# A transformer pair on one core: the recurrent scan as a pipeline over pairs of heads, fewer columns in 16 linear tiles, and the last projection computed by rows

## The reference

```python
def _wkv7_scan(r, w, k, v, a, b):          # 16 heads of 64, over 272 tokens
    def step(S, inp):
        sa = einsum('bhvk,bhk->bhv', S, a_t)
        S = S * w_t[:, :, None, :] + sa[..., None] * b_t[:, :, None, :] + v_t[..., None] * k_t[:, :, None, :]
        return S, einsum('bhvk,bhk->bhv', S, r_t)
...
z_rwkv = z_rwkv + (z_prev - z_rwkv) * mu           # r, k, v and three small inputs
y_b = _fox(z_fox, q_g, k_g, f_bias)                # softmax attention with a decay bias
merged = g_a * (y_a @ w_a) + g_b * (y_b @ w_b)
h = h + merged @ w_o
gate, up = jnp.split(_rms(h, n2) @ w_gu, 2, axis=-1)
return h + (jax.nn.silu(gate) * up) @ w_dn         # the last projection, "down2"
```

## Time and profile before

| | us |
|---|---|
| median of three runs (2892.56 to 2895.17) | 2893.81 |
| the profiled execution | 2892.87 |
| its span | 2890.8 |
| PE busy in the span | 2856.2 |
| DVE busy | 1735.4 |
| ACT busy | 1223.3 |
| all waits of PE in the view of waits (15 rows) | 27.1 |

### The profile page before, as it was taken

One profiled execution on the slowest core, in us unless ns is written; L12 is line 12 of the kernel. 1 busy time (PEld: TensorE's weight loads), 2 busy tenths in 40 slices (PEclk: granted clock), 3 DMA queues, 4 the chain that ended last, 5 costly groups with the idle time before them and its releaser, 6 DMA issues.

```text
span 2890.8 us, 55153 instructions
## 1 busy us (share of the span) xinstructions
PE 2856.2 (99%) x23517; PEld 2629.2 (91%) x23517; DVE 1735.4 (60%) x2522; ACT 1223.3 (42%) x1788; POOL 53.0 (2%) x102
## 2 busy tenths in 40 slices
PE   9999999999999999999999999999999999999999
PEld 8999998888888999899888888899998888889999
DVE  6467757656566444754666665766666566655444
ACT  5345544333333344633433333455453333334343
POOL 1000000000000000000000000000000000000000
PEclk9999999999999999999999999999999999999999
DMA  7666445565555555455434335445555555555553
GB/s 245 199 168 167 156 163 172 177 190 187 188 189 175 190 187 189 153 167 168 118 88 118 102 89 160 132 123 184 180 186 188 182 183 187 189 189 183 182 188 131
DMA packets 370328, 485.21 MB, mean 168 GB/s; under 512 B 12359, under 2 KB 181654, under 8 KB 370150
## 3 DMA queue, kind: packets, MB, share of 16 engines
q1 hardware_dynamic: 362752, 471.55, 51.6%
q0 software_dynamic: 4112, 7.88, 0.9%
q10 hardware_dynamic: 3302, 3.39, 0.4%
HBM read 475.76 MB, written 7.01 MB: 167 GB/s over the span
## 4 chain that ended last, share of the span: by engine, by line
PE 91%; DVE 6%; issue 1%; ACT 1%; DMA 1%; DVEq 0%; SPq 0%; ACTq 0%
PE psum L338 20%; PE psum L344 12%; PE psum L342 12%; PE psum L343 12%; PE psum L340 10%; PE psum L543 6%; PE psum L547 5%; PE psum L545 5%; DVE w_lo L328 2%; PE psum L1796 1%; DVE arena L716 1%; PE psum L1782 1%; DVE arena L704 0%; PE psum L2612 0%; DVE act L791 0%
## 5 line engine op out<-in xcount | busy, mean ns | idle before, releaser
L328 DVE TENSOR_TENSOR w_lo<-w_raw,w_hi 128x1024 fp32r<-128x1024 f32 x728 | 859.0, 1221 | 797.6 <-ACT w_hi L319 797.6
L319 ACT ACTIVATE w_hi<-w_raw 128x1024 fp32r<-128x1024 f32 x728 | 731.4, 1052 | 1161.8 <-PE psum L340 591.5
L338 PE MATMUL psum<-act,w_hi 128*128 128x512 f32 x2816 | 989.6, 394 | 8.9 <-issue 4.5
L342 PE MATMUL psum<-act,w_hi 128*128 128x256 f32 (+2 forms) x3024 | 854.7, 283 | 6.9 <-issue 4.5
L344 PE MATMUL psum<-act,w_lo 128*128 128x256 f32 (+2 forms) x3024 | 855.6, 283 | 0.0
L343 PE MATMUL psum<-act,w_hi 128*128 128x256 f32 (+2 forms) x3024 | 855.6, 283 | 0.0
L340 PE MATMUL psum<-act,w_lo 128*128 128x256 f32 x2816 | 790.7, 281 | 0.0
L338 PEld LDWEIGHTS psum<-act,w_hi 128*128 128x128 f32 x2816 | 529.6, 188 | 136.8 <-DVE w_lo L328 11.2
L342 PEld LDWEIGHTS psum<-act,w_hi 128*128 128x128 f32 (+1 forms) x3024 | 571.6, 189 | 11.3 <-issue 8.3
L344 PEld LDWEIGHTS psum<-act,w_lo 128*128 128x128 f32 (+1 forms) x3024 | 572.2, 189 | 0.0
L343 PEld LDWEIGHTS psum<-act,w_hi 128*128 128x128 f32 (+1 forms) x3024 | 568.4, 188 | 0.1
(11 more groups left out here) (391 smaller groups left out, 1584.8 us busy)
## 6 DMA issues: line engine op xcount, KB each, us to landing
w_raw<-w_in SPq DMA_DIRECT2D x128, 1024.0 KB, 5.7
w_raw<-w_down SPq DMA_DIRECT2D x88, 1024.0 KB, 5.0
w_raw<-w_gate_up SPq DMA_DIRECT2D x88, 1024.0 KB, 5.0
w_raw<-w_gate SPq DMA_DIRECT2D x44, 1024.0 KB, 5.2
w_raw<-w_up SPq DMA_DIRECT2D x44, 1024.0 KB, 5.2
w_raw<-w_out SPq DMA_DIRECT2D x16, 1024.0 KB, 5.0
w_raw<-w_o SPq DMA_DIRECT2D x16, 1024.0 KB, 5.0
w_raw<-w_branch_a SPq DMA_DIRECT2D x8, 1024.0 KB, 5.0
```

Of the source, the lines that this page charges most:

```text
L319: nc.scalar.activation(w_hi[:, s % 2, 2 * h:2 * h + 2, 0:wd], w_raw[:, s % RAW, 2 * h:2 * h + 2, 0:wd], ACT.Copy).then_inc(hi_ready, 1)
L328: nc.vector.tensor_tensor(w_lo[:, s % 2, 2 * h:2 * h + 2, 0:wd], w_raw[:, s % RAW, 2 * h:2 * h + 2, 0:wd], w_hi[:, s % 2, 2 * h:2 * h + 2, ...
L338: pe.matmul(dst.rearrange("p (h n) -> p h n", h=2), w1, both_parts, start=first, stop=False, skip_group_check=True)
L342: pe.matmul(dst, w1, act_hi[:, k, tok], start=first, stop=False, skip_group_check=True)
```

## The change

The scan becomes a pipeline over pairs: x, u, y of pair j - 1 stand between the products of the inverse of pair j, and an epilogue does those of pair 7. The Gram matrices with r and with k are made behind the joins, the part that the joins need is made small beside the blocks ("near"). Tokens, decay factors and the inverse have two buffers. In the scan ACT now copies u. r and its decayed form take the place of r and k in `z`. Tiles of r ("rkv", the first eight) get 258 columns in place of 272, the first eight fox tiles 256. The last projection keeps the activations stationary and moves 512 weight columns, with the residual added by a float32 matmul against the identity.

The diff, cut to its core:

```diff
+        R_TOK = slice(META - 2, TOK)
+        def r_tiles(lin, i):
+            return lin is L["rkv"] and isinstance(i, int) and i < 2
...
+        def fox_tok(t):
+            return X if t < 8 else ALL
...
+        def rows_pe(lin, lo_base):
+            def residual(s):
+                for b in range(2):
+                    for j in range(4):
+                        pe.matmul(psum[:, 2 * s + b, j * P:(j + 1) * P],
+                                  res[:, 4 * s + j, META + b * P:META + (b + 1) * P], ident,
+                                  start=j == 0, stop=False, skip_group_check=True)
...
+                for s in range(4):
+                    if first:
+                        if s < 2:
+                            pe.wait_ge(acc_free, lin.t0 - 2 + 2 * s)
+                        residual(s)
+                    pe.wait_ge(lo_ready, 2 * u + 2)
+                    for b in range(2):
+                        for k in range(UNIT_K):
+                            pe.matmul(out_rows, x1, w1, start=False, stop=False, skip_group_check=True)
+                            pe.matmul(out_rows, x1, w0, start=False, stop=False, skip_group_check=True)
+                            mm = pe.matmul(out_rows, x0, w1, start=False, stop=last and k == UNIT_K - 1,
+                                           skip_group_check=True)
...
+            def gram_r(j, c):        # bh by r alone: 128 columns for a half, where gram(0, c) had 256
+                for h, r in enumerate(hs):
+                    pe.matmul(o[low], bh[r, t0:t1], r_of[r, t0:t0 + P], start=True, stop=True)
...
+                side(4)
+                if j:
+                    pe.wait_ge(*rd.after(("x128", before)))
+                    pe.wait_ge(*ra.after(("x128", before)))
+                    pe.wait_ge(*rd.after(("gram_r", before)))
+                    front(j)
+                side(4)
...
                 product(4, n8t, n8, "p2")
-                gram(0, 0)
+                if j:
+                    chunk_x(before, 0)
                 dve("ip2")
                 product(5, ip2, i8t, "r1t")
                 act("p2")
                 product(4, p2t, p2, "p4")
-                gram(0, 1)
+                if j:
+                    chunk_u(before, 0)
                 dve("ip4")
                 act("r1t")
                 product(4, r1t, ip4, "s8")
-                gram(1, 0)
+                if j:
+                    act("near")
+                    chunk_y(before, 0)
                 dve("s8t")
                 product(5, nm16, s8t, "v16")
-                gram(1, 1)
+                side(1)
                 act("v16")
                 product(4, v16, s8, "s16")
-                side(1)
+                if j:
+                    chunk_x(before, 1)
                 dve("s16t")
                 product(5, nm32, s16t, "v32", 4)
-                side(1)
+                if j:
+                    chunk_u(before, 1)
                 act("v32")
                 product(4, v32, s16, "s32", 4)
-                side(1)
+                if j:
+                    chunk_y(before, 1)
...
-            down_pe(L["down2"], LO_BASE["down2"], lambda s: s > 1 and end_transpose(s - 2))
-            end_transpose(2)
-            end_transpose(3)
+            rows_pe(L["down2"], LO_BASE["down2"])
```

More of the change, by code:

```diff
@@ L1590, in zt, with ar_of @@
             return z[:, n, 1:ZP]
+        def ar_of(j):
+            return z[:, j:j + 9:8, 1:ZP]
         lora_w = (LORA, LORA, P, P)
@@ new lines, in chunk_x @@
+            def chunk_x(j, c):
+                toks = toks_s[j % 2]
+                pe.wait_ge(*rd.after((f"sh{c + 1}", j)))
+                pe.wait_ge(*rd.after(("gram_k", j)))
+                for h in range(2):
+                    pe.matmul(psum[:, 0, hs[h]], gm[:, 2 * h + c, 2 * P:3 * P], toks[:, 2 + c, hs[h]],
+                              start=h == 0, stop=False, skip_group_check=True)
+                pe.matmul(psum[:, 0, 0:P], ar_of(j)[:, 0, PIECES[c + 1]], state_h.rearrange("p h v -> p (h v)"),
+                          start=False, stop=True, skip_group_check=True) \
+                    .then_inc(*rp.did((f"x{c + 1}", j)))
@@ L1792, in product, with center @@
+            def center(j):
+                pe.wait_ge(*rd.after(("ys", j)))
+                pe.matmul(psum[:, 2, 0:SEQ], T["head_center"], ys, start=True, stop=True) \
+                    .then_inc(*rp.did(("yc", j)))
+            front(0)
+            for j in range(8):
+                before = j - 1
+                inv_t = inv_ts[j % 2]
+                dve, act = lambda n: pe.wait_ge(*rd.after((n, j))), lambda n: pe.wait_ge(*ra.after((n, j)))
                 def product(bank, l, r_, step, nq=5):
@@ L1843, in rwkv_pe @@
                 mm.then_inc(*rp.did(("x64", j)))
+                dve("x0")
+                for h in range(2):
+                    mm = pe.matmul(psum[rows32(h), 2, 0:RHD], s16[rows32(h), 4], xs[rows32(h), 0],
+                                   start=True, stop=True)
+                mm.then_inc(*rp.did(("u0", j)))
+                if j:
+                    pe.wait_ge(*rd.after(("ys", before)))
+                gram_r(j, 0)
+                gram_r(j, 1)
                 side(1)
-                low, high = slice(0, 64), slice(64, P)
                 dve("x64t")
@@ L2026, in rwkv_act, with copy, u_copy @@
             table(ACT.Tanh)
+            def copy(dst, src):
+                return s.activation(dst, src, ACT.Copy)
+            def u_copy(j, c):
+                s.wait_ge(*rp.after((f"u{c}", j)))
+                copy(us, psum[:, 1, 0:P].rearrange("p (h v) -> p h v", h=2)).then_inc(*ra.did((f"u{c}", j)))
             for j in range(8):
@@ L2052, in rwkv_act @@
                 ins.then_inc(*ra.did(("toks", j)))
-                side(6)
-                def copy(dst, src):
-                    return s.activation(dst, src, ACT.Copy)
+                side(7)
                 def evac(step, of, dst, bank, nq=5):
```

637 lines of the change are left out of this document (371 added, 266 removed).

## The result

The changed kernel took 2912.27 us (median of 4 runs, 2905.82 to 2916.43) beside 2893.18 us for the kernel before (4 runs, 2890.67 to 2895.17). The ratio is 1.006, its interval 1.0042 to 1.0077: slower, where 2885 us (2874 to 2895) was predicted. All readings are of the execution of 2905.82 us, span 2903.7; before it was 2892.9 and 2890.8, so 12.9 us of span have to be found. It is the shortest of the four, with a mean granted clock of 0.991 over the execution; the longest, 2916.43 us, has 0.988, so the time of one program moves with its clock.

A forecast was written before the change was run, and what follows sets the result against it. PE, under way for 99% of the span, was taken as the bound. Scan -13, columns -5.1, last projection +0.3 and fox +9 gave -8.8: 2892.9 to 2884.1 us profiled, 2885 against the median, range 2874 to 2895.

The forecast's parts named there:

- The clock: Low clock expected only after the idle stretch at fox's end, with matmuls twice as far apart, priced at 1.7 us.
- the three rivals: Fox's end costs only 3 us (chance 0.2); pairs save only entries (0.2); joins stand open, kernel at 2904 (0.1).
- The pairs: Scan: each pair 2.0 us shorter, 16 us for eight, from entries, exits, grams and small groups, less new waits.
- Entries and exits: Scan, per pair: 11 fewer slot bursts save 1.16 us; fewer changes of shape after slots save 0.28.
- The other 0.3 for the grams and 0.3 for the ends of small groups: Scan, per pair: halved gram calls less "near" save 0.3 us; merged small groups without drains save 0.3.
- New waits: Scan joins, chunks replacing slots and grams: 0.6 us of idleness a pair against 0.4 before, 0.2 more.
- the second rival: Scan: pairs save only the entries, 1.0 to 1.2 us a pair; 2892 in all, no change; chance 0.2.
- The edges of the scan: Pair 0's open joins and pair 7's chunks behind it, less what pairs 0 and 1 lack: net 3 us dearer.
- The end of fox: Pair 7 of fox lacks slots: waits 6.7 us late, second unit 0.5, low clock 1.7; +9 us in all.
- Columns: Narrower tiles save 2.4 us in r and 2.7 in fox; -5.1 us together (-4 to -6).
- The last stage: Last projection: main matmuls -3.6 us, residual +7.6, transposes -1.8, end -1.8; together +0.3 (-3 to +3).
- The third part: Last projection: transposes no longer needed save 1.8 us, and a shorter end saves 1.8.

The follow-up runs named there:

- experiment 1: Changed kernel with six of the ten slots around pair 0's blocks moved into its open joins; 2898.22 us, ratio 1.0015.
- experiment 6: experiment 5 with pair 7's four slots ahead of the inverse moved into its joins; 2886.38 us, ratio 0.9971.
- experiment 5: Changed kernel with six slots back in pair 0's joins and 0 instead of 2 slots behind each fox output; 2890.25 us, ratio 0.9997.
- experiment 9: Kernel before with only the edits outside the scan: columns of r and fox, and rows of the last stage; 2885.09 us, ratio 0.9971.
- experiments 2 and 3: Changed kernel with pair 0's six joins filled with unused work: full-array matmuls (2), 2907.57 us; 32 by 32 matmuls (3), 2921.22 us.
- experiment 11: The changed kernel itself, unaltered, measured once more; 2903.06 us, ratio 1.0034.

## Why the prediction was wrong, by its own steps

**The clock, the step that failed most.** The prediction read the 99% of the earlier trace rows as a PE that stays fast whatever the order, priced a low clock at 1.7 us in fox's end, and let pair 0's joins stand open for 3.0 us of plain waiting. The open joins cost 9.1 us (experiment 1), of which some 8 are the clock; pair 7's stretch and the next 4.2 (experiment 6 beside 5, both stages). The prediction also took matmuls at the lower level as twice as far apart, where they are 1.8 times. With the clock the scan is +9.7 us; without these 12.2 us it would be -2.5. The had shown that PE at 1.2 GHz is 5 us of waiting away, and the same reading was not applied to the joins. None of the three rivals had it.

The Trainium skill, TensorE: Matmul & The Clock Gate, section "What's actually happening", says that the clock gate follows how busy the array has been. The traces agree if busy is not read as the share of time that PE is under way: at the beginning of fox in experiment 1 the clock falls at 1813.74 behind 10.00 us of 10.00 under way (clock: third from the end).

```profile
1803.74:1813.74 10.00, 10.00 (x75) 7.92 (x74) 5.48 (x13) 6.12 (x6) 0.00 (x0) 1.00 0.41 107
1813.74:1817.15 3.41, 3.41 (x18) 3.41 (x18) 0.41 (x2) 0.63 (x1) 0.00 (x0) 0.50 0.59 155
```

What ends just before it are 3.2 us of float32 matmuls with 16 or 128 moving columns. Within the pairs, in contrast, every fall had 0.87 us or more of idle time in the 5 us before it.

**The pairs: -2.0 us each, measured -0.5.** Compare pairs 1 to 6 in experiments 5 and 9, which differ only in the order of the scan and are both at full clock (sums of the intervals from start to start, all six pairs):

```
                                  old order   new order    a pair
slots, entries and exits              159.9       150.0     -1.64
products                               22.2        22.5     +0.05
x: L1939 / L1905                       5.26        5.94     +0.11
x: L1941 / L1907                       2.35        4.44     +0.35
u: L1948 / L1916                       4.35        7.06     +0.45
grams, with near                       14.2        14.2      0.00
all others                             61.0        62.0     +0.17
all                                   269.2       266.1     -0.51
```

Entries and exits were right: 126 bursts became 60, 1.64 us where 1.44 was forecast. But the chunks took 0.91 back, and the prediction had only 0.57 for the changes of shape, hidden in the term "exits". The timeline of PE, changed kernel, pair 2:

```profile
1512.54 0.52 PE L1958 MATMUL psum<-arena 32*32 32x32 f32 x36
1512.99 0.66 PE L1905 MATMUL psum<-arena 128*128 128x64 f32 x4
1513.49 0.44 PE L1907 MATMUL psum<-arena 128*128 128x128 f32 x2
1513.86 0.85 PE L1958 MATMUL psum<-arena 32*32 32x32 f32 x72
1514.63 0.66 PE L1916 MATMUL psum<-arena,tab 128*128 128x64 f32 x4
1515.22 0.52 PE L1958 MATMUL psum<-arena 32*32 32x32 f32 x36
```

x takes 0.50 + 0.37 = 0.87 us between products, u 0.59; behind a slot they took 0.39 + 0.20 and 0.36. A full-array group between two 32 by 32 groups pays on both sides, some 0.1 going in and 0.17 coming out. The other 0.3 for the grams and 0.3 for the ends of small groups did not show. New waits were small, as predicted (PE's idle time in these six pairs is 1.0 us in experiment 5 and 1.7 in 9). This is the second rival's result ("the pairs save only the entries", 1.0 to 1.2 us a pair), reached by another road and at half its size.

**The edges of the scan** were forecast as 3 us dearer. Pair 0, which now has no chunk, is 4.1 us shorter in experiment 5 than in 9 when its five more slots (3.5 us) are put apart, and pair 7's chunks outside cost 16.2 (65.3 - 49.1) - 7.8 (11 slots) - 3.5 (clock, experiment 6) = 4.9: +0.8 net with pair 0's joins filled, where the forecast's 3 us were for open ones.

**The end of fox: +9 us, measured +9.0.** Timeline of PE, changed kernel:

```profile
1951.37 0.87 PE L2830 MATMUL psum<-tab,inv 128*128 128x144 f32 x4
...
1958.93 1.11 PE L2856 MATMUL psum<-arena 16*64 16x256 f32 x4 [4.89 <-ACT arena L2731]
...
1965.56 0.65 PE L2856 MATMUL psum<-arena 16*64 16x256 f32 x4 [1.46 <-ACT arena L2725]
...
1967.34 0.58 PE L342 MATMUL psum<-act,w_hi 128*128 128x256 f32 x1 [0.32 <-DVE act L833]
```

The count of slots, the wait of 4.9 us for the copy of the weights (7.56 us behind scores(7), where 7.5 were forecast from the earlier trace rows), the second wait and the low clock all came as written. Another 1.7 us of low clock fell on "branch".

**Columns: -5.1 us, right.** The part ahead of pair 0 is 2.7 us shorter; by the forecast's price it would be 3.3, 2.4 for r and 0.9 for the 20 fox slots that stand there. The other 44 narrower slots lie in pairs 0 and 1, which experiment 9 has 2.2 us shorter than before (1.9 forecast). Its pairs 2 to 6 are another 1.9 us shorter with the same columns, 1.3 of it idle time of PE.

**The last stage: +0.3 us, measured -2.9.** The main matmuls were mis-sized. Before, 256 columns start 0.1185 us apart, the mean over the stage, not 0.1179 as the earlier trace rows gave; after, 512 start 0.232 apart, as forecast: 5.4 us less, where 3.6 was taken. The residual is cheaper: four times 1.70 us, 6.8 in place of 7.6. The timeline of PE at its first step:

```profile
2648.39 1.95 PE L695 MATMUL psum<-tab,res 128*128 128x128 f32 x16
2650.09 0.48 PE L716 MATMUL psum<-w_hi,act 128*128 128x512 f32 x1
```

The third part, the transposes and the end, came to 4.3 us for its 3.6.

**The sum by these terms**: -13 became +9.7, -5.1 became -4.6, +0.3 became -2.9, +9 became +10.7 with the echo on "branch". With the scan's 12.2 us of clock out, the change would have stood at +0.7, no change (an estimate). The clock alone doesn't bridge the way to -8.8: the pairs' 1.5 us each, 9 us in six of them, are the other step that failed.

## What to carry to other kernels

On a PE-bound kernel, ask of every reordering what the array sees for the next microseconds, not only how many microseconds of queue it saves: wide matmuls between small-tile products do two jobs, covering waits and keeping the clock up, and a stretch left without them can make the slots behind it cost 1.8 times as much. Price a group by its neighbours on both sides; a burst saved is worth nothing if a group of another shape takes its place. Reorderings that move the clock should be tried one at a time: here some 20 us lost in the scan and around fox's end hid 7.5 us of sound gains elsewhere.

## What was unexpected of the hardware

- The granted clock fell behind a stretch in which PE was under way 10.00 us of 10.00 (experiment 1, 1813.74 us), 3.2 us of matmuls with 16 and 128 columns at its end.
- Idle pieces much shorter than the 4.5 us of the earlier trace rows stood ahead of falls: 0.74 and 0.42 us and part of a third in pair 0 of the changed kernel, one of 1.20 us in pair 7 of experiment 5. Gaps put down to "issue" have no cause that the profile shows, and they vary: the one behind the fall in pair 0 is 0.89 us in one profile of the changed kernel, and in the other one of 2.05 us ends 0.7 us ahead of the fall.
- Moving three slots a pair by some microseconds turned a kernel whose profile has no fall in the scan into one with a fall in each of eight pairs, 95.6 us in all.
- The same instructions in pairs 1 to 6 fell in some programs (pair 5 in experiments 2 and 3, pair 6 in 3) and not in others, each time behind a gap of 0.87 to 1.50 us put down to "issue". Such gaps also came without a fall (0.94 us in pair 0 of the kernel before, 1.17 us in experiment 11). What sets this is open: the experiments show which orders are at risk, not where the limit lies.
- Of the price, 3.4 or 6.8 us at half clock cost little; the 17 to 24 us stretches came where the joins and what followed them had few wide matmuls.
